# A hybrid attention layer on one core: the weight loads of the step stage move from SyncE's queue to ScalarE's queue

## The reference, cut to what matters

```
h   = rmsnorm(x, norm_pre_g)
u   = h @ w_in                      # 1024 x 4096, eight column groups of 512:
dq, dk, dv, dg, mq, mk, mv, mg = split(u)
A   = differential attention (4 heads): softmax(q0 k0) - lam * softmax(q1 k1), times v, rmsnorm per head
B   = block attention (8 heads): with 512 rows and blocks of 256 every past block is chosen: causal softmax
y   = concat(A * silu(dg), B * silu(mg)) @ w_out       # 1024 x 1024
out = x + rmsnorm(y, norm_post_g)
```

## Time and profile before

| | us |
|---|---|
| median of 3 runs | 261.27 (260.73 to 262.19) |
| profiled execution | 263.27 |
| its span on the core | 261.5 |
| TensorE busy in the span | 249.4 (95%) |
| VectorE busy | 177.5 (68%) |
| ScalarE busy | 143.5 (55%) |
| loads of weights | 40 of 512.0 KB, 4.4 (w_in) and 3.8 (w_out) from issue to landing |
| transposes of probabilities | 32, 3.6 from issue to landing |

### The profile page before, as it was taken

The page is one execution under the profiler, slowest core; times in us unless marked ns, Lnnn a source line. Parts: engine busy times, 40 slices in busy tenths (PEclk is TensorE's granted clock), DMA queues, the critical chain, the costliest instruction groups (busy, mean ns, idle before and its releaser), DMA issues.

```text
span 261.5 us, 4394 instructions
## 1 busy us (share of the span) xinstructions
PE 249.4 (95%) x1581; PEld 123.3 (47%) x1581; DVE 177.5 (68%) x383; ACT 143.5 (55%) x335; POOL 30.4 (12%) x76
## 2 busy tenths in 40 slices
PE   7689999999999999999999989999999999999990
PEld 7445444444444544544455434444544444554440
DVE  2587785338849688798678576875698786934223
ACT  3784973236546475685475685665645675721111
POOL 2059000000000050050004014000000000110101
PEclk9999999999999999999999999999999999999998
DMA  6994697297415343753422864576907739999404
GB/s 220 385 311 116 193 345 235 82 345 237 116 36 131 93 112 100 197 128 102 120 84 61 176 139 147 125 193 153 168 13 143 140 60 173 220 194 261 120 3 162
DMA packets 55402, 41.42 MB, mean 158 GB/s; under 512 B 41536, under 2 KB 41800, under 8 KB 55380
## 3 DMA queue, kind: packets, MB, share of 16 engines
q1 hardware_dynamic: 55380, 41.14, 59.5%
HBM read 29.04 MB, written 2.13 MB: 119 GB/s over the span
## 4 chain that ended last, share of the span: by engine, by line
PE 82%; DVE 6%; ACT 5%; DMA 3%; issue 2%; POOL 1%; SPq 0%; DVEq 0%; POOLq 0%; ACTq 0%
PE unit_ps L510 71%; PE score_ps L529 5%; PE o_ps L549 5%; DMA stage<-in_w_in_dram 3%; DVE w_lo L732 2%; ACT arena L649 1%; DVE w_lo L730 1%; ACT junk L595 1%; ACT w_hi L609 1%; DVE v_lo L773 1%; PE score_ps L471 1%; ACT area L641 1%; ACT w_hi L608 1%; DVE arena L822 0%; DVE area L788 0%
## 5 line engine op out<-in xcount | busy, mean ns | idle before, releaser
L510 PE MATMUL unit_ps<-w_hi,area 128*128 128x512 f16 x256 | 80.7, 379 | 3.6 <-DVE area L788 2.3
L510 PE MATMUL unit_ps<-area,w_hi 128*128 128x512 f16 x256 | 76.2, 379 | 0.0
L649 ACT ACTIVATE arena<-arena,negmax 128x512 f32<-128x512 f32 (+3 forms) x64 | 35.4, 554 | 48.4 <-DVE negmax L802 48.1
L510 PE MATMUL unit_ps<-area,w_lo 128*128 128x512 f16 x128 | 48.5, 379 | 0.0
L510 PE MATMUL unit_ps<-w_lo,area 128*128 128x512 f16 x128 | 48.5, 379 | 0.0
L510 PEld LDWEIGHTS unit_ps<-w_hi,area 128*128 128x128 f16 x256 | 25.0, 98 | 34.1 <-DVE area L788 2.7
L510 PEld LDWEIGHTS unit_ps<-area,w_hi 128*128 128x128 f16 x256 | 23.8, 98 | 26.5 <-issue 0.8
L802 DVE CUSTOM_DVE_ANT_0 arena<-score_ps,strips 128x512 f32<-128x512 f32 (+3 forms) x64 | 28.6, 484 | 8.6 <-PE score_ps L529 8.6
L730 DVE SCALAR_TENSOR_TENSOR w_lo<-stage,g_cols,w_hi 128x512 f16<-128x512 f32 x32 | 24.1, 754 | 11.4 <-ACT w_hi L609 11.3
L608 ACT ACTIVATE w_hi<-stage,g_cols 128x512 f16<-128x512 f32 x32 | 22.7, 710 | 5.1 <-DMA stage<-in_w_in_dram 5.1
L732 DVE SCALAR_TENSOR_TENSOR w_lo<-stage,g_cols,w_hi 128x512 f16<-128x512 f32 x32 | 24.8, 776 | 0.0
(11 more groups left out here) (78 smaller groups left out, 314.7 us busy)
## 6 DMA issues: line engine op xcount, KB each, us to landing
stage<-in_w_in_dram SPq DMA_DIRECT2D x32, 512.0 KB, 4.4
stage<-in_w_out_dram SPq DMA_DIRECT2D x8, 512.0 KB, 3.8
arena<-in_x_dram SPq DMA_DIRECT2D x4, 512.0 KB, 9.7
strips<-bias_rows SPq DMA_DIRECT2D x1, 2048.0 KB, 8.9
stage<-in_x_dram SPq DMA_DIRECT2D x4, 512.0 KB, 4.4
out_dram<-area SPq DMA_DIRECT2D x3, 512.0 KB, 2.7
strips<-bias_rows SPq DMA_DIRECT2D x1, 1024.0 KB, 5.7
g_row<-in_norm_post_g_dram SPq DMA_DIRECT2D x1, 512.0 KB, 10.3
```

The lines of the kernel that those rows point to most:

```text
L510: last = nc.tensor.matmul(bank, a, b, start=(k == 0 and n == 0), stop=(k == KT - 1 and n == 2))
L649: nc.scalar.activation(probs[:, i % 2, m, 0:n], probs[:, i % 2, m, 0:n], ACT.Exp, bias=negmax[:, i, m:m + 1], scale=-1.0, accum_out=sums[: ...
```

## The change

`load_quarter` moves out of SyncE's block and takes the queue as an argument. The loads ahead of the steps stay on SyncE. In the slots, SyncE issues none any more. ScalarE issues the load that follows split n, one slot after that split, behind `exps(j)` and ahead of its own next `split`.

```diff
+        def load_quarter(queue, n):
+            if n >= 4:
+                queue.wait_ge(split_lo, n - 3)
...
+            queue.dma_start(stage[:, n % 4, :].rearrange("p (k n) -> p k n", k=2), src)\
+                .then_inc(w_loaded[n % 4], 16)
...
         @block.sync
...
                 for t, half in TURN_SLOT.get(j, []):
                     turn_a(t, half)
-                for n in SPLIT_IN_SLOT[j]:
-                    if n + 4 < QUARTERS:
-                        load_quarter(n + 4)
                 if j in XRES_SLOT:
...
         @block.scalar
...
                 if j < NSTEP:
                     exps(j)
+                for n in SPLIT_IN_SLOT[j - 1] if j else ():
+                    if n + 4 < QUARTERS:
+                        load_quarter(act, n + 4)
                 for t, half in TURN_SLOT.get(j, []):
                     a_hi(t, half)
                 for n in SPLIT_IN_SLOT[j]:
```

More of the change, by code:

```diff
@@ L304, in bass_hymba_diff_moba_layer @@
         diff_normed = sem("diff_normed")
+        def load_quarter(queue, n):
+            if n >= 4:
+                queue.wait_ge(split_lo, n - 3)
+            g, k = n // 4, 2 * (n % 4)
+            if g < len(GROUPS):
+                col = GROUPS[g][2]
+                src = w_in_v[:, k:k + 2, col:col + WIDTH]
+            else:
+                col = (g - len(GROUPS)) * WIDTH
+                src = w_out_v[:, k:k + 2, col:col + WIDTH]
+            queue.dma_start(stage[:, n % 4, :].rearrange("p (k n) -> p k n", k=2), src)\
+                .then_inc(w_loaded[n % 4], 16)
         block = ctx.enter_context(nc.Block())
@@ L310, in _ @@
         def _(sp):
[L311 to L322, removed]
             def turn_probs(i):
@@ L350, in _ @@
             sp.dma_start(g_rows[:, :], norm_pre_g[0].rearrange("(k p) -> k p", p=P)).then_inc(gpre_loaded, 16)
-            load_quarter(0)
-            load_quarter(1)
+            load_quarter(sp, 0)
+            load_quarter(sp, 1)
             load_x(1)
-            load_quarter(2)
-            load_quarter(3)
+            load_quarter(sp, 2)
+            load_quarter(sp, 3)
             load_x(2)
@@ L362, in _ @@
             for n in range(4, 9):
-                load_quarter(n)
+                load_quarter(sp, n)
             sp.wait_ge(row_built, 1)
@@ L369, in _ @@
                 for n in SPLIT_AT_UNIT[u]:
-                    load_quarter(n + 4)
+                    load_quarter(sp, n + 4)
             sp.dma_start(strips[:, DIFF_HEADS:HEADS, :], strip_view(DIFF_HEADS, HEADS)).then_inc(strips_loaded[1], 16)
```

## The result

The changed kernel takes 263.85 us, the median of 8 runs (262.77 to 265.91). The kernel before, run beside it, takes 261.51 us (8 runs, 260.73 to 262.39). The ratio is 1.0104, with a 95% interval of 1.0078 to 1.0129: **the change costs about 2.3 us, and the kernel is slower**. The forecast of 261.9 us was too low. The time lies in its range all the same, in the case called "The transposes land late in every slot" (263.3 to 264.9 us).

What follows compares the result with a forecast made beforehand. The prediction took TensorE to bound the kernel, waiting only for transposes in the changed stage. It summed +0.4 us (step 20) and +0.2 us (step 0) to +0.6 us, from 261.27 to 261.9 us, range 260.5 to 265.2 us.

Steps and rivals of the forecast that it cites:

- The transposes land late in every slot: Rival: load and transpose leave together and share DMA engines; step 20 +2.0, step 0 up to 1.6 us; 263.3 to 264.9; chance 0.15.
- the rival of the held-up issue: ScalarE's load issues wait for SyncE's transposes, in nearly every slot; 264.6 to 267 us, 265 in the middle; chance 0.22.
- the sum: Main case: +0.4 us at step 20 and +0.2 at step 0, giving +0.6 us, 261.9 us; chance 0.42 within the bound.
- the gap at 152.9: TensorE's 0.74 us wait ahead of values(16), put down to a late transpose; expected to close, its gain swallowed by step 20.
- Taking the issues off SyncE is worth nothing: Removing 22 issues of 0.37 us, 8.2 us, and their waits from SyncE's stream gains nothing by itself.
- The added wait for `split_lo`: ScalarE's wait ahead of each of 22 load issues; claimed always met already, since exps(j) waited for later logits.
- 0.3 us per issue on ScalarE: Assumed cost of each load issue in ScalarE's stream, between bounds of zero and 0.37 us; five in slots 16 to 20.
- 1.1 us late at step 20: Transpose of step 20 delayed by five issues, 1.5 us less 0.38 hidden; landing 172.4 against 171.97, TensorE 0.4 us later.
- the ring: Slots 16 to 20: ScalarE and VectorE wait on each other through logits, exponentials, `w_hi`, `w_lo`; added issue time there is paid.
- Behind instead of ahead of the transpose: Each load leaves about 2 us later, behind the next transpose; step 16's then lands after 3.6 us, bounds 2.5 and 5.3.
- Step 0: Its load moves from 1.6 us ahead of the transpose to about the same time; +0.2 us, between -0.1 and +1.6.
- issue hides: Rival: the issue runs beside the exponentials, step 20 is not late, the 0.74 us gap closes; 260.5 to 260.7 us; chance 0.15.

Runs made afterwards that it cites:

- act_tiny_issues: The kernel before, loads still on SyncE, plus two 8 KB transfers issued by ScalarE at each of the change's 22 load places; 263.81 us, ratio 1.0110.

## Why the prediction was right and where it was wrong

**The number.** That 263.85 us lies in the range is not the merit of the sum, which gave 261.9 us and put its own case at 262.6 us at most. It is luck: the range reached to 265.2 us for the rival of the held-up issue, and no run shows that mechanism in the changed kernel.

**What bounds the kernel: right.** TensorE sets the pace, and waits only for transposes; the gap at 152.9 was a transpose behind a load, not the VectorE instruction named in the row. The run without loads takes that gap away (as does the load behind the transpose). The new waits came at steps 0 and 20, the two named as near the edge, and at 15 and 16.

**Taking the issues off SyncE is worth nothing: right.** SyncE's stream with and without the 22 issues gives the same time where the moment is the same: 1.0080 and 1.0104 just ahead of the transpose, 0.9980 and 0.9999 behind it. Neither pair speaks for a gain from the second queue.

**The added wait for `split_lo`, and the loads' own users: right.** No split waited for a load.

**The term "0.3 us per issue on ScalarE": wrong, it is 0.** The upper bound of 0.37 was the right duration; the lower bound, zero, was the right price. The step that failed is the reason I gave for the lower bound: I allowed the issue only the 0.1 us of overlap between neighbours in ScalarE's stream, and so took a value near the upper end. The row of after shows it issued 0.22 us into the first exponential. With it the "1.1 us late at step 20" through the ring did not exist: the transpose of step 20 was issued at 167.1 in a profile whose steps started 1.5 us earlier (55.54 against 54.02), which is 1.1 us later than before in the steps' own time. That is the very lateness that I forecast, by luck: it is TensorE's own lag from steps 0, 15 and 16, which stood at 1.04 us at values(19). I had said that step 20 is set by the ring and not by TensorE; but the ring waits for TensorE in slot 20, now 1.51 us instead of the 1.19 of the earlier trace rows, and so takes over TensorE's lag. The row's start, 164.40 - 54.02 = 110.38 against 164.87 - 55.54 = 109.33 before, is 1.05 us later, as TensorE is. No run took the waits at steps 0 and 15 away alone, so the path is read from the rows and not tried. The row of after, ScalarE in slot 20:

```profile
164.40 0.60 ACT L625 ACTIVATE strips<-unit_ps 128x512 f32<-128x512 f32 x1 [1.51 <-PE unit_ps L507]
```

**"Behind instead of ahead of the transpose": wrong, and this decided the size.** The prediction took the place in the program for the moment. Behind exps(j) in the code, I had the load leave at 148, behind the transpose of 147.45, and land the transpose of step 16 after 3.6 us. It left ahead of the transpose, by 0.37 us, because the stream runs ahead of the engine. Of the bounds given for that landing (2.5 and 5.3), the upper one came, and a little more: 5.7 us. The lower one, taken from step 3, was not to be had either: without any load this transpose lands after 3.2 us. So the gap at step 16 did not close (1.02 us, before 1.21), and step 20 landed after 5.5 us.

**Step 0: right in kind, too small.** I gave it 0.2 us, with an upper bound of 1.6; the wait went from 0.57 to 1.29 us, 0.7 more.

**Rival "issue held up": not seen.** All 22 issues of the changed kernel took 0.37 us, and of the pairs of act_tiny_issues those that met a transpose took as long (0.44 us) as those that did not, but for a few. The Trainium skill's rule that led to 265 us ("Perfetto Trace Analysis", "DMA Instruction — HWDGE (DVE, Sync)": each DMA instruction locks the descriptor generator for itself) may hold, but then the lock is not held for the 1.19 us of a transpose.

**Rival "issue hides": half right.** The issue hides, and the gain that was to follow from it was eaten by the late landings.

**Rival "transposes land late in every slot": this is what happened, in most slots.** 263.3 to 264.9 were named, 263.85 was measured. That the number fits so well is in part luck. The rival's sum for step 20 has the 1.1 us of late issue in it, which came from TensorE's lag and not from ScalarE's issues; and the median landing was 4.3 us and not 5.3. I had held against it that landings were mostly 2.5 to 3.7 us where the load was over a microsecond ahead. That is true of the kernel before (median 3.3), but the changed kernel's loads are not there. Its companion from the skill ("DMA: Bandwidth & Descriptors", "Issuing engines are not separate DMA queues": DMAs of all engines interleave on the same 16 DMA engines, and only issuing time is saved) agrees with the table above. I had written that it would not change the sum; it did, by the place of the load and not by the gap.

## What to carry to other kernels

Where a small transfer that something waits for and a bulk load are issued near each other, put the bulk load right **behind** the small one: 512 KB issued about 0.4 us ahead cost the transpose 1.6 us of landing in the median (4.3 against 2.7), issued 1.3 us behind from the same queue they cost it nothing that shows in the median (from ScalarE's queue 0.4 us, and no time of the kernel). Which engine issues the load matters little. On ScalarE a DMA leaves when the last semaphore wait ahead of it in the program is met, and not when the computing ahead of it is done. If the moment matters, move the DMA across a wait, or give it a semaphore of its own.

## What the hardware showed that I had not expected

- ScalarE issues DMAs ahead of its own pending compute: 0.22 us into an exponential that stands ahead of it, and 0.46 us before a split that stands ahead of it. It does not pass a wait: all 22 loads left 0.04 us after the logits that the exponentials ahead of them wait for. One such issue of 0.33 us a slot is free (ratio 1.0006 for 22 of them); with a second one right behind it VectorE's wait grew by 0.37 us.
- Two issues at the same moment on ScalarE's and SyncE's queues took 0.45 and 1.19 us, within 0.01 us what each took without the other (0.44 for the second of a pair on ScalarE, 1.19 for a transpose).
- The 16 DMA engines were busy for 0.50 to 0.62 of the time in the stretches shown, so there was room on the average, and still a transpose behind a load landed up to 3.0 us later than that of the same step without loads (step 1, 5.4 against 2.4 us). The average does not show what is in front of a transfer at its moment.
